# Output projection by token tile: the last four weight units at five stage ends

## The reference, cut to what matters

```
x = x + mixer_ab(x, ...)                      # layer 0; layer 1: conformer_conv
x = x + cross_attn(x, mem, norm, ..., wo)     # ends in  o @ wo
x = x + conv_ffn(x, norm, ..., w_down)        # ends in  (gelu(g) * u) @ w_down

def rms_norm_2(x, g):
    y = x * lax.rsqrt(jnp.mean(x * x, axis=-1, keepdims=True) + EPS)
    return y * g
```

## Time and profile before

| | |
|---|---|
| median of three runs | 1900.85 us |
| profiled execution, its own time | 1901.49 us |
| its span | 1899.2 us |
| TensorE busy | 1768.4 us, 93% |
| VectorE busy | 1228.9 us, 65% |
| ScalarE busy | 1021.7 us, 54% |
| mean granted clock of TensorE | 0.961 |
| issues that load weights from the largest group, 512 KB each | 224, 3.6 us to landing |

### The profile page before, as it was taken

How to read it: one execution, slowest core, us unless ns; L and a number is a source line. 1 busy time by engine, 2 the same in 40 slices (tenths; PEclk the granted TensorE clock), 3 DMA queues, 4 the chain that set the end, 5 groups by cost and what they waited for, 6 DMA issues and landing times. The chain is left out here.

```text
span 1899.2 us, 26521 instructions
## 1 busy us (share of the span) xinstructions
PE 1768.4 (93%) x10480; PEld 1571.8 (83%) x10480; DVE 1228.9 (65%) x1661; ACT 1021.7 (54%) x1390; POOL 32.9 (2%) x59
## 2 busy tenths in 40 slices
PE   7999999999999999999999899999999118989998
PEld 7888888888888888888889788999999007889997
DVE  5755767667656566755867755665565995556655
ACT  6845557454666455645465755644465005555443
POOL 5000000000000000000000000000000000000000
PEclk9989999999998999999999999999999558999999
DMA  8535555566663655556656453566656003446663
GB/s 268 158 109 178 171 167 156 177 189 202 183 181 103 175 166 163 156 175 190 196 181 181 156 181 119 177 183 187 185 178 189 22 0 112 130 136 188 183 187 120
DMA packets 161946, 306.74 MB, mean 162 GB/s; under 512 B 12346, under 2 KB 16356, under 8 KB 161696
## 3 DMA queue, kind: packets, MB, share of 16 engines
q1 hardware_dynamic: 158928, 298.91, 52.2%
q0 software_dynamic: 2896, 6.15, 1.0%
HBM read 303.97 MB, written 1.05 MB: 161 GB/s over the span
## 5 line engine op out<-in xcount | busy, mean ns | idle before, releaser
L929 DVE TENSOR_TENSOR weights_lo<-weights_raw,weights_hi 128x1024 fp32r<-128x1024 f32 x562 | 672.7, 1223 | 468.4 <-ACT weights_hi L490 465.1
L490 ACT ACTIVATE weights_hi<-weights_raw 128x1024 fp32r<-128x1024 f32 x562 | 580.9, 1054 | 491.5 <-DMA weights_raw<-in_w_in_dram 186.1
L1487 PE MATMUL bank<-h_hi,weights_hi 128*128 128x256 f32 x1504 | 429.2, 285 | 10.5 <-DVE weights_lo L929 5.2
L1487 PE MATMUL bank<-h_hi,weights_lo 128*128 128x256 f32 x1504 | 427.6, 284 | 0.0
L1487 PE MATMUL bank<-h_lo,weights_hi 128*128 128x256 f32 x1504 | 427.4, 284 | 0.0
L1469 PE MATMUL bank<-weights_hi,h_hi 128*128 128x512 f32 x928 | 366.9, 395 | 6.3 <-ACT arena L907 6.3
L1469 PE MATMUL bank<-weights_lo,h_hi 128*128 128x512 f32 x928 | 363.5, 392 | 0.0
L1469 PE MATMUL bank<-weights_hi,h_lo 128*128 128x512 f32 x928 | 363.5, 392 | 0.0
L1487 PEld LDWEIGHTS bank<-h_hi,weights_hi 128*128 128x128 f32 x1504 | 290.7, 193 | 12.8 <-DVE weights_lo L929 5.0
L1469 PE MATMUL bank<-weights_hi,arena_parts 128*128 128x512 f32 x928 | 292.3, 390 | 1.6 <-DVE weights_lo L929 1.6
L1487 PEld LDWEIGHTS bank<-h_hi,weights_lo 128*128 128x128 f32 x1504 | 290.8, 193 | 0.5
(11 more groups left out here) (289 smaller groups left out, 1499.3 us busy)
## 6 DMA issues: line engine op xcount, KB each, us to landing
weights_raw<-in_w_in_dram SPq DMA_DIRECT2D x224, 512.0 KB, 3.6
weights_raw<-in_f_w_up_dram SPq DMA_DIRECT2D x96, 512.0 KB, 3.9
weights_raw<-in_f_w_down_dram SPq DMA_DIRECT2D x48, 512.0 KB, 3.7
weights_raw<-in_w_up_dram SPq DMA_DIRECT2D x40, 512.0 KB, 3.7
weights_raw<-in_c_w_pw_dram SPq DMA_DIRECT2D x24, 512.0 KB, 3.6
weights_raw<-in_ab_w_in_dram SPq DMA_DIRECT2D x20, 512.0 KB, 3.6
weights_raw<-in_w_mem_kv_dram SPq DMA_DIRECT2D x16, 512.0 KB, 3.6
weights_raw<-in_w_out_dram SPq DMA_DIRECT2D x16, 512.0 KB, 3.7
```

The lines of the kernel that those rows point to most:

```text
L490: nc.scalar.activation(w_hi[:, q % SPLIT, 0:w], raw[:, n % RAW, 0:w], ACT.Copy).then_inc(hi_done, 1)
L929: tt(w_lo[:, n % RAW, 0:w], raw[:, n % RAW, 0:w], w_hi[:, q % SPLIT, 0:w].bitcast(F32), ALU.subtract)\
L1487: ins = mm(bs[i][:, j, :], wp[:, kk, f * P:(f + 1) * P], sp_[:, 2 * u + kk, :], start=first and u == us[0] and kk == 0 and n == 0 and j == ...
```

## The change

The last two units of each half (four units: n = 0 and 1, two units each) are multiplied at five stage ends (AB, X0, F0, X1, F1) by a new function `by_token`: first all four for token tile 0, then all four for token tile 1. A unit is marked as done by its product for tile 1. In F0 and F1 these four are the whole of the last `down`. The number of products and what is accumulated stay. `pieces` now gives the order by token tile at these ends, so the residual additions and the squares come as (n, t) = (0, 0), (1, 0), (0, 1), (1, 1) instead of (0, 0), (0, 1), (1, 0), (1, 1). Stage C keeps the old order, and L0 and L1 already had the new order of `pieces`.

```diff
         def pieces(prev):
 
-            return [(n, t) for t in range(NT) for n in range(2)] if prev[0] == "L" else [(n, t) for n in range(2) for t in range(NT)]
+            return [(n, t) for n in range(2) for t in range(NT)] if prev == "C" else [(n, t) for t in range(NT) for n in range(2)]
...
             def residual():
-                for n, t in pieces("X"):
-                    b = filled("o", 2 * n + t, 2 if n else None)
+                for n, t in pieces(VC.stage):
+                    b = filled("o", 2 * n + t, 2 if n + t else None)
...
+            def by_token(name, src, us, ready):
+
+                ws = []
+                for t in range(NT):
+                    for n in range(2):
+                        for u in us:
+                            if t == 0:
+                                ws.append((at[0], unit(2, W)))
+                                if ready and n == 0:
+                                    pe.wait_ge(vec_done, VC.at(ready % u if "%" in ready else ready))
+                            number, w = ws[2 * n + us.index(u)]
+                            for kk in range(2):
+                                for m, (wp, sp_) in enumerate(passes(w, src)):
+                                    ins = mm(bank(PC, name, 2 * n + t)[:, :], sp_[:, 2 * u + kk, t * P:(t + 1) * P], wp[:, kk, :],
+                                             start=False, stop=u == us[-1] and kk == 1 and m == 2)
+                            tile = [(name, 2 * n + t)] if u == us[-1] else []
+                            if t:
+                                ins.then_inc(pe_done, PC(*tile))
+                                PC.marks["unit", number] = PC.n
+                            elif tile:
+                                end(ins, *tile[0])
...
-            for n in range(2):
-                proj_T("o", 2 * n, us=(2, 3), first=False, ready="ya1lo")
+            by_token("o", H_HL, (2, 3), "ya1lo")
...
-                for n in range(2):
-                    proj_T("o", 2 * n, us=(2, 3), first=False, ready="o_lo%d")
+                by_token("o", H_HL, (2, 3), "o_lo%d")
...
                 def down(j):
+                    if j == 5:
+                        by_token("o", F_HL[1], (0, 1), "h5lo")
+                        return
                     for n in range(2):
-                        proj_T("o", 2 * n, src=F_HL[j % 2], us=(0, 1), first=j == 0, last=j == 5, ready=f"h{j}lo")
+                        proj_T("o", 2 * n, src=F_HL[j % 2], us=(0, 1), first=j == 0, last=False, ready=f"h{j}lo")
```

## The result

| | before | after | ratio |
|---|---|---|---|
| first measurement, median of 10 and 10 | 1900.38 us | 1905.66 us (1901.1 to 1906.19) | 1.0024 [1.0015, 1.0034] |
| second measurement, median of 33 and 11 | 1900.17 us | 1903.58 us (1903.31 to 1904.33) | 1.0017 [1.0009, 1.0026] |
| profiled execution, span | 1899.2 us | 1898.8 us | |

The change makes the kernel slower by 3.4 to 5.3 us by medians (3.4 and 4.6 us by means), against 1904.2 us and +3.3 us forecast. Both medians lie in the range. Both intervals have the bound of 0.2% inside them, so whether the change is "within" or "over" stays undecided; that it is slower is not in doubt.

What follows compares the result with a forecast made beforehand. TensorE, busy 93% of the span, was taken to bound the kernel. Stalls of 0.65 + 0.65, 1.06 behind X1 and 0.93 at the end sum to 3.3 us on the median 1900.85: 1904.2 us, range 1902.0 to 1906.2.

Steps and rivals of the forecast that it cites:

- Part 1: ScalarE's norm order: two squares behind the waiting root of t0; normalised t1 0.76 us later, the end's pair 0.93 us later.
- Part 2: Unit N's weight slot given back 4.09 us later, so the split of N+6 is late; addition of o(1,1) 0.30 us later.
- Part 3: Behind X0 and F0: `k` waits for the bank of o(0,1), now added third; TensorE stands 0.65 us at each.
- nothing gives them back: Behind X0 and F0: the two 0.65 us stalls lie on TensorE's own path, so both count in full.
- Part 4: Stage ends: covered AB, X0, F0 show nothing of 1.06 us (X0 slack 1.78); X1 loses 1.06, F1 0.93.
- The first rival: Covered ends AB, X0, F0: slack used up, each paying at most 1.06 us; 6.5 us in all, 1907.3 us; chance 0.10.
- the sign that was named: Behind X1: F1's first product 1.06 us later against X1's last product.
- The clock: Behind X1: idle time grows by 1.06 us; no change in clock cost taken, bounds -1.2 and +1.2 us.
- the second rival: Behind X1: one more stretch at the lower clock, 3.3 + 1.2 = 4.5 us, 1905.4 us; chance 0.13.
- Rivals 3 and 4: Third: no bank stall before `k`, 2.0 us stay, 1902.8 us, chance 0.13. Fourth: early token helps, -1.6, 1899.3 us, chance 0.06.
- rival 4: X1 and the end: t0's `base` and root done while t1 is multiplied, 0.8 us sooner at each, -1.6; chance 0.06.

Runs made afterwards that it cites:

- The square early: Changed kernel, but at the five ends ScalarE squares o(0,1) ahead of the first root, so one square stands between the roots: 1903.58 us, 1.0015 against before.
- three edits (bank, split, order with products): Changed kernel with `k` in other banks, 1903.76 us; with N+6 split behind the additions, 1902.15; with only products in the new order, additions and squares in the old, 1901.85.
- the fillers: 12 and 7 products on old data put into TensorE's two idle times behind X1, in both kernels: before 1898.16 us, changed 1901.6 us.
- the products alone: Kernel before with only TensorE's products in the new order, residual additions and squares in the old one: 1901.85 us, 1.0007 against before.
- order alone: Kernel before with only residual additions and squares in the new order, products in the old one: 1903.38 us, 1.0017 against before.
- the filled kernel before: Kernel before with 12 useless products ahead of F1's transposes and 7 behind them, in TensorE's idle time: 1898.16 us, 0.9987 against before.
- The early token: Changed kernel, N+6 split behind the norm, VectorE issuing `base` and normalisation of t0 right behind its two additions: 1897.6 us, 0.9987 against before.

## Why the prediction was right, step by step

- **Part 1, the root that waits.** Right in place and size. Two squares stand behind root t0, `base` of t1 waits 1.49 us, the end loses 0.95 (0.93 forecast). The square early takes exactly this away (3.42 at the end).
- **Part 2, slots given back later.** Right. The high part of N+6 starts 3.59 us before X0's last product (1177.80 to 1181.39); the forecast's 1181.85 against 1185.44 is the same 3.59. The chain from it to the additions (1.09, 1.15, 0.72 each) came as worked out. At AB, X0, F0 and X1 TensorE is the releaser.
- **Part 3, the bank.** The stall is right: 0.65 behind F0 as forecast, 0.80 behind X0. At X0 `k` starts 0.26 us behind the end of the third addition (1180.04 + 2 x 0.72 + 0.69 = 1182.17, and 1182.43), at F0 0.10. In between the trace has two wait instructions in TensorE's queue at X0 (1182.21 for the bank, 1182.32 for the unit's splits) and none at F0; that they are the other 0.15 us is likely, but not tested. Each of three edits (bank, split, order with products) makes the stall go. Wrong, in these traces, is "nothing gives them back": X0's is kept, but F0's 0.65 us don't show in the distance from F0's last product to X1's last, 275.33 us in after and 275.58 in before; over the twelve traces it is 275.0 to 275.5 with the stall and 274.9 to 275.8 without. The cause is open. The forecast has a term of 0.65 in its sum there that the whole distances don't have.
- **Part 4, covers.** Right: no idle time ahead of X0's transposes, nor of F0's. The first rival fell. Behind X1 t1's normalisation moved from 3.42 to 4.49 us behind the last product, 1.07 (1.06 forecast). The wait, which ends with t0's, grew by 1.17. But the sign that was named, F1's first product 1.06 us later, came out at 2.14 (10.25 and 8.11), because the transposes ran at the lower clock; with the fillers it is 1.15 (9.17 and 8.02).
- **The clock.** This is a term that was sized wrong: it was put at zero, with 1.2 us as the bound. The traces of after and of the products alone and order alone have 10.24 us at the lower level behind X1, where before has 6.83, and in after that is 0.9 us beside the wait. That is the second rival, in the traces. Its length isn't the price, though: the second trace of after has two stretches of 3.41 us, in all as much as before, and loses 2.2 us at X1 all the same. What it costs an average execution these runs can't fix: without fillers the change costs 3.4 and 4.6 us by means, with them 3.7, all give or take 1.7 or more. The Trainium skill (TensorE: Matmul & The Clock Gate, HAM oscillation) says that idle gaps put the array back to half rate and that this is paid anew at each restart; the filled kernel before agrees, with no lower clock behind X1 and 1.9 us less by medians (1900.06 and 1898.16).
- **Rivals 3 and 4.** No stall before `k`: fell by the rows. The early token: fell for this change, since VectorE's rows didn't move; as an edit of its own it gives 1.5 us at its two places in the trace, where rival 4 has 1.6, and 2.5 by medians.
- **Luck in the sum.** The 3.3 us come close to the measured 3.4 to 5.3, and the chains behind them are shown. But two terms that the sum has wrong have opposite signs and nearly the same size in the traces: the clock behind X1, left out (0.9), and F0's stall, counted in full (0.65). That 1904.2 lies between the two medians owes something to that.

## What to carry to other kernels

Finishing one tile early by reordering products gained nothing here until the queues behind it were reordered too: read, for each engine, what stands behind the last wait, since an early operation moved behind a later wait becomes a late one. When several units are used twice in place of one after the other, ask when their slots come free and which bank the next stage takes first. An idle time of TensorE that grows can be paid a second time in the clock; products on dead data in that idle time are cheap and were worth about as much here as the early token (1.9 and 2.5 us by medians). And a stall removed on the busiest engine need not come back in the time: look at the distance to a product far behind it, past the next stage in which that engine idles.

## What was not expected of the hardware

- The two traces of the changed kernel differ by 2.8 us at a point which the change hardly touches. Over all twelve traces X0's last product started between 1181.39 and 1186.05 us, which is about the size of the whole effect. Stretches at the lower clock fall elsewhere each time. A comparison of single executions at 0.2% is worthless without aligning them at one product.
- 19 products of no use (12 in 2.88 us and 7 in 1.86 us of TensorE) made the kernel before faster, 0.9987 [0.9979, 0.9996]. From X1's last product to 200 products into F1 they saved 33.57 - 32.09 = 1.5 us; the granted clock there was 1.00 throughout. Only 0.09 us of it lies ahead of F1's first product (8.11 and 8.02 us behind X1's last): the slower transposes were hidden there, and the saving is in the products of F1.
- An idle time of 0.49 to 0.64 us ahead of `k` left no mark in the clock: the products behind it kept their 0.12 us distance.
